# Expert weights dealt to partitions in runs of neighbouring rows, and the transposes that go with it

## The chip, the cores and the metric

One core of a Trainium2 chip runs the whole program. The metric is the device time of one execution in microseconds (us), the median of several; lower is better. Before the change it is 2893.73 us (three runs, 2891.6 to 2898.68).

## The reference

One layer of a decoder trunk for a prompt of 1024 tokens and 8 sample tokens (1032 tokens of 1024 features, all in float32): layer norm, adaptive modulation, an input projection, two mixing branches (a short gated convolution and a state-space scan), a merge, a second layer norm, and then a mixture of 32 experts, of which each token uses two. The change is in the experts alone. A token's features `xblk` meet two weight matrices of its expert:

```python
D_MODEL, D_EXPERT, N_EXPERTS, MOE_BLOCK = 1024, 512, 32, 128
# w_moe_13: (N_EXPERTS, D_MODEL, 2 * D_EXPERT)     w_moe_2: (N_EXPERTS, D_EXPERT, D_MODEL)
def expert_block(args):
    xblk, e = args
    gate, up = jnp.split(xblk @ w13[e], 2, axis=-1)
    return (jax.nn.silu(gate) * up) @ w2[e]
```

The tokens are sorted by expert into blocks of up to 128, and the two results of a token are added with their router weights. What is summed over is the feature axis (1024 in the first product, 512 in the second); the order of that sum is free.

## The kernel before

The program is written by hand for the five engines, each with its own list of instructions and semaphores between them; no scheduler moves anything. Up to about 2087 us it does the norms, projections, convolution, scan and merge. Then the router picks the experts (to about 2150 us), and the expert loop runs until about 2800 us: one turn for each block of 128 gathered token rows, 32 turns in the profiled run. After it the results are gathered back, scaled, normed and stored.

The weights of an expert are 6 MB: `w_moe_13[e]` is 1024 x 1024, loaded in four parts of 1 MB (`load_w13`, L635), and `w_moe_2[e]` is 512 x 1024, loaded in two (`load_w2`, L639). Part x of the first holds the 256 feature rows 256x to 256x + 255: row (2x + k) * 128 + p goes to partition p, column block k (k = 0, 1). So each partition gets two runs of 4 KB (one row of 1024 float32 each), and the part as a whole is one block of 1 MB in memory. SP issues all these loads; six buffers (`wraw`, called u_whole or arena in the rows) take them, and SP issues the next load into a buffer when DVE has last read it (`wlo_ready`).

Each raw part is split into two float32r halves: ACT copies it (`w_high`, L1062), DVE subtracts (`w_low`, L1559); a ring of three split buffers (we_parts) passes them to TensorE, which gives a buffer back with `wparts_used`. TensorE makes three matmuls for each product (high x high, high x low, low x high), in `gate_up` (L2092 to L2094) and `down` (L2110, L2113, L2114).

The token rows come by an indirect DMA from POOL into `xg` (tokens on partitions). TensorE wants the features on partitions, so it transposes them in blocks of 128 columns: `turn_rows` (L2079) makes four transposes into bank 6 for each half, and for each half ACT copies the result (`x_high`, L1067) and DVE takes the low part (`x_low`, L1661). The product h = silu(gate) * up (`silu` on ACT, L1071; DVE, L1666) is transposed in the same way by `turn_h` (L2120, four transposes into bank 7; `h_high` L1075, `h_low` L1670). Transpose k takes columns k * 128 to k * 128 + 127, the features of the rows that column block k of the weights holds. In a transpose the block that is turned is the loaded operand (LDWEIGHTS, shown as PEld), and the identity matrix is the one that is streamed (MATMUL, shown as PE).

TensorE's order in a turn n (`expert_turn`): the first half of gate/up part 0 of block n, `turn_h` of block n - 1, the second half of that part, `down` of block n - 1, gate/up part 1, the first half of the next token rows (`turn_rows`), part 2, the second half of them, part 3. ACT's order: `silu`, `w_high` 2, `h_high`, `w_high` 3 and 4, the two output copies (L1082, L1083) and their store, `w_high` 5, `x_high` of the first half, `w_high` 0 of the next block, `x_high` of the second half, `w_high` 1. DVE's: the product h, `h_low`, `w_low` 2 to 5, `x_low`, `w_low` 0, `x_low`, `w_low` 1.

Of the kernel before, what the change touches and what calls it, by code (L numbers as in the profile page):

```python
# [25 lines left out]
ds = bass.ds  # L26

P = 128
D = 1024
KD = D // P  # L30
# [69 lines left out]
def build(nc, t, o):  # L100
# [3 lines left out]
    with ctx:  # L104
        def sem(name):
            return ctx.enter_context(nc.semaphore(name))
# [24 lines left out]
        bank6, bank7 = pair[:, 0:512], pair[:, 512:1024]  # L131
# [7 lines left out]
        class Room:  # L139
# [5 lines left out]
            def take(self, n):  # L145
# [13 lines left out]
        ident = keep.take(P)  # L159
# [153 lines left out]
        hm = [r5.take(D_EXP) for _ in range(2)]  # L313
        xg = [r5.take(D), wflat[6]]
# [15 lines left out]
        wraw = [u_whole[:, 0:2 * D], w2_raw, r5.take(2 * D)] + [u_whole[:, 2 * D * x:2 * D * x + 2 * D]  # L330
                                                               for x in range(1, 4)]
# [52 lines left out]
        wraw_landed = [sem(f"wraw_landed{j}") for j in range(6)]  # L384
# [32 lines left out]
        def tile_rows(ap, i):  # L417
            return ap[i * P:(i + 1) * P, :] if i < TILES else ap[SEQ:TOK, :]

        w13_v = t["w_moe_13"][0].rearrange("e (k p) c -> p (e k) c", p=P)  # L420
        w2_v = t["w_moe_2"][0].rearrange("e (k p) c -> p (e k) c", p=P)

        def slots_before(n):

# [14 lines left out]
        def _(sp):  # L439
# [143 lines left out]
            with sp.Fori(0, 3) as i:  # L583
                c = sp.snap(i * 256)
# [47 lines left out]


            def load_w13(j, x, expert):
                sp.dma_start(wraw[j].rearrange("p (k c) -> p k c", k=2),  # L635
                             w13_v[:, ds(expert * KD + 2 * x, 2), :]).then_inc(wraw_landed[j], 16)

            def load_w2(x, expert):
                sp.dma_start(wraw[1 + x].rearrange("p (k c) -> p k c", k=2),  # L639
                             w2_v[:, ds(expert * 4 + 2 * x, 2), :]).then_inc(wraw_landed[1 + x], 16)  # L640


            sp.wait_ge(wo_done, TILES + 1)
            for x, j in enumerate((0, 3, 4, 5)):
                load_w13(j, x, 0)
            sp.wait_ge(x0_used, TILES + 1)
            load_w2(0, 0)
            sp.wait_ge(logits_done, 1)
            load_w2(1, 0)
            for x, j in enumerate((0, 3, 4, 5)):  # L650
                sp.wait_ge(wlo_ready, x + 1)
                load_w13(j, x, 1)
# [4 lines left out]
            def expert_of(n):  # L657
                return sp.value_load(plan[:, ds(n, 1)], min_val=0, max_val=EXPERTS - 1)

            with sp.Fori(0, extra + (PAIRS - 1)) as i:  # L660
                for b in range(2):
                    n = i * 2 + (b + 2)
                    before, expert = expert_of(i * 2 + (b + 1)), expert_of(i * 2 + (b + 2))
                    for j in range(6):
                        sp.wait_ge(wlo_ready, i * 12 + (6 * b + 5 + j))
                        if j in (1, 2):
                            load_w2(j - 1, before)
                        else:
                            load_w13(j, max(j - 2, 0), expert)
            expert = expert_of(extra * 2 + (2 * PAIRS - 1))  # L670
# [1066 lines left out]
        def _(pe):  # L1737
            pe.wait_ge(consts_ready, 1)
            pe.wait_ge(c_landed, 32)
            for k in range(KD):  # L1740
                last = pe.transpose(bank6[:, k * MROWS:(k + 1) * MROWS], crow[:, k * P:(k + 1) * P],
                                    ident[0:MROWS, 0:MROWS])
# [25 lines left out]
            for k in range(16):  # L1768
                last = pe.transpose(bank6[:, k * MROWS:(k + 1) * MROWS], mod[:, k * P:(k + 1) * P],
                                    ident[0:MROWS, 0:MROWS])  # L1770
# [3 lines left out]
            for k in range(KD):  # L1774
                last = pe.transpose(bank6[:, k * ROWS_C:(k + 1) * ROWS_C], rows_c[:, k * P:(k + 1) * P],
                                    ident[0:ROWS_C, 0:ROWS_C])
            last.then_inc(cols_turned, 1)
            for half in range(2):
                pe.wait_ge(cols_copied, 2 + half)
                for k in range(16):  # L1780
                    kk = 16 * half + k
                    last = pe.transpose(bank6[:, k * ROWS_S:(k + 1) * ROWS_S], rows_s[:, kk * P:(kk + 1) * P],
                                        ident[0:ROWS_S, 0:ROWS_S])
# [9 lines left out]
            for i in range(TILES + 1):  # L1793
                rows = P if i < TILES else NS
                for k in range(KD):
                    last = pe.matmul(bank7[0:rows, i * HEADS:(i + 1) * HEADS], uT[:, k, i * P:i * P + rows],
                                     w_dt[:, k, :], start=(k == 0), stop=(k == KD - 1))
# [242 lines left out]
            for i in range(TILES + 1):  # L2040
# [3 lines left out]
                for half in range(2):  # L2044
                    for k in range(KD):
                        last = pe.matmul(banks[2 * (i % 2) + half][0:rows, :], merged[:, k, i * P:i * P + rows],  # L2046
                                         w_o[:, k, 512 * half:512 * half + 512], start=(k == 0), stop=(k == KD - 1))
# [17 lines left out]
            for a in range(2 * NI):  # L2065
                last = pe.matmul(banks[4][:, 0:NBX], oh_lo[:, a, :], oh_hi[:, a, :], start=(a == 0),
                                 stop=(a == 2 * NI - 1))
# [3 lines left out]
            def turn_rows(b, n, half, landed):  # L2071

                if half == 0:
                    pe.wait_ge(xg_landed[b], landed)
                if not (isinstance(n, int) and n == 0 and half == 0):
                    pe.wait_ge(xt_ready, n * 2 + half)
                for k in range(4):
                    kk = 4 * half + k
                    last = pe.transpose(bank6[:, k * P:(k + 1) * P], xg[b][:, kk * P:(kk + 1) * P], ident)  # L2079
                last.then_inc(xg_turned, 1)  # L2080

            def gate_up(b, n, x, j, ks=(0, 1)):
# [34 lines left out]
            def turn_h(b, n):  # L2117
                pe.wait_ge(h_ready, n + 1)
                for k in range(4):
                    last = pe.transpose(bank7[:, k * P:(k + 1) * P], hm[b][:, k * P:(k + 1) * P], ident)  # L2120
                last.then_inc(ht_turned, 1)

            def expert_turn(b, n, landed):


                first = isinstance(n, int) and n == 0
                pe.wait_ge(xt_ready, n * 2 + 2)
                if first:
                    gate_up(b, n, 0, 0).then_inc(wparts_used, 1)
                else:  # L2130
                    if not (isinstance(n, int) and n == 1):
                        pe.wait_ge(h_ready, n - 1)
                    gate_up(b, n, 0, 0, (0,))
                    turn_h(1 - b, n - 1)
                    gate_up(b, n, 0, 0, (1,)).then_inc(wparts_used, 1)
                    if not (isinstance(n, int) and n == 1):
                        pe.wait_ge(o_free, n * 2 - 2)
                    down(1 - b, n - 1, 0, 2, n * 6).then_inc(wparts_used, 1)
                    down(1 - b, n - 1, 1, 0, n * 6 + 1).then_inc(wparts_used, 1)
                skip = 0 if first else 2  # L2140
                gate_up(b, n, 1, 1 + skip).then_inc(wparts_used, 1)
                turn_rows(1 - b, n + 1, 0, landed)
                gate_up(b, n, 2, 2 + skip).then_inc(wparts_used, 1)
                turn_rows(1 - b, n + 1, 1, landed)
                gate_up(b, n, 3, 3 + skip).then_inc(wparts_used, 1)
# [3 lines left out]
            for half in range(2):  # L2149
                turn_rows(0, 0, half, 16)  # L2150
            expert_turn(0, 0, 16)
            expert_turn(1, 1, 32)
            with pe.Fori(0, extra + (PAIRS - 1)) as i:
                expert_turn(0, i * 2 + 2, i * 16 + 32)
                expert_turn(1, i * 2 + 3, i * 16 + 48)
            turn_h(1, extra * 2 + (2 * PAIRS - 1))
            pe.wait_ge(o_free, extra * 4 + (4 * PAIRS - 2))
            down(1, extra * 2 + (2 * PAIRS - 1), 0, 2, extra * 12 + (12 * PAIRS)).then_inc(wparts_used, 1)
# [28 lines left out]
```

## Time and profile before

| | before |
|---|---|
| median of 3 runs | 2893.73 us (2891.6 to 2898.68) |
| the profiled execution | 2899.79 us, of it 2898.0 us from first to last instruction |
| mean granted TensorE clock | 0.952 |
| PE / PEld busy | 2587.1 us (89%) / 1892.4 us (65%) |
| DVE / ACT / POOL busy | 1506.0 us (52%) / 1051.9 us (36%) / 287.9 us (10%) |
| DMA | 405.11 MB, mean 140 GB/s |

The page describes this one execution. Its busy shares are means over stages that work differently, so the expert loop has to be looked at by itself: by the windows from 2184 to 2798 us. A "wait" in the tables is idle time of an engine and what ended it; the chain is followed back from an end to what released each step. PE's rows are matmuls, PEld's the loads of the operand that stays in the array.

### The profile page before, as it was taken

Reading aid. Unit: us, or ns where it says so; the run is one execution under the profiler, and the core shown is the slowest. Engines: PE = TensorE matmul, PEld = TensorE weight load, DVE = VectorE, ACT = ScalarE, POOL = GpSimd, SP = SyncE. Lnnn points to the kernel's source line nnn. Section 1 sums busy time; section 2 is a strip of 40 time slices with the busy share of each in tenths; the row PEclk is TensorE's granted clock in tenths of the full one; section 3 lists DMA queues with packets and bytes.
Section 4 is the critical chain, followed back from the end, with each engine's and each line's share of the span. In section 5 each row is a group of like instructions: output and inputs, shape, how many; then the busy total and the mean of one; then the engine's idle time right before and its main releaser. Section 6 shows DMA issues by size and latency. Waiting matters only on the chain.

```text
span 2898.0 us, 34179 instructions
## 1 busy us (share of the span) xinstructions
PE 2587.1 (89%) x11876; PEld 1892.4 (65%) x11876; DVE 1506.0 (52%) x2335; ACT 1051.9 (36%) x1338; POOL 287.9 (10%) x218
## 2 busy tenths in 40 slices
PE   6999999999999976899999999999949898988960
PEld 2376666666666644677789998875437777777750
DVE  3332576666765766100012331115557777777769
ACT  0212645535446445200000000000027777777751
POOL 0000000000000000111133441110000000000011
PEclk9889999999999988999999999999969999999985
DMA  8733222222222111111111112121239999999964
GB/s 272 260 117 102 74 62 60 69 71 64 62 68 71 55 39 33 46 44 43 43 31 51 43 50 103 44 54 66 102 119 352 368 358 361 364 356 368 362 242 142
DMA packets 253304, 405.11 MB, mean 140 GB/s; under 512 B 13273, under 2 KB 163425, under 8 KB 253161
## 3 DMA queue, kind: packets, MB, share of 16 engines
q1 hardware_dynamic: 227936, 327.72, 33.6%
q0 software_dynamic: 11744, 43.35, 4.1%
q10 hardware_dynamic: 13536, 33.04, 3.3%
q8 instruction: 35, 0.57, 0.1%
q14 instruction: 53, 0.43, 0.0%
HBM read 356.21 MB, written 48.15 MB: 140 GB/s over the span
## 4 chain that ended last, share of the span: by engine, by line
PE 41%; DVE 6%; issue 6%; ACT 5%; DMA 1%; ACTq 1%; DVEq 0%; POOL 0%; POOLq 0%; SPq 0%
PE bank L1974 11%; PE bank L1936 5%; PE bank L1938 5%; PE bank L1937 5%; PE bank L2046 4%; ACT we_parts L1062 4%; PE bank L2113 2%; PE bank L2110 2%; PE bank L2114 2%; DVE we_parts L1559 2%; PE bank L2079 1%; PE bank L2120 1%; DVE arena L1666 1%; DVE x_parts L1661 1%; ACT arena L1083 1%
## 5 line engine op out<-in xcount | busy, mean ns | idle before, releaser
L1810 PE MATMUL bank<-u_whole,arena 128*128 128x344 f32 x2304 | 693.0, 457 | 0.0
L1810 PEld LDWEIGHTS bank<-u_whole,arena 128*128 128x128 f32 x2304 | 436.2, 192 | 220.6 <-issue 15.0
L1559 DVE TENSOR_TENSOR we_parts<-u_whole,we_parts 128x2048 fp32r<-128x2048 f32 x129 | 295.1, 2287 | 79.2 <-ACT we_parts L1062 79.2
L1936 PE MATMUL bank<-u_parts,w_parts 128*128 128x344 f32 x960 | 313.0, 326 | 14.4 <-DVE u_parts L1418 7.3
L1937 PE MATMUL bank<-u_parts,w_parts 128*128 128x344 f32 x960 | 307.8, 321 | 0.0
L1974 PE MATMUL bank<-arena 128*128 128x344 f32 x1056 | 307.8, 452 | 0.0
L1938 PE MATMUL bank<-u_parts,w_parts 128*128 128x344 f32 x960 | 307.7, 321 | 0.0
L1062 ACT ACTIVATE we_parts<-u_whole 128x2048 fp32r<-128x2048 f32 x129 | 246.9, 1915 | 70.4 <-PE bank L2110 27.0
L1974 PEld LDWEIGHTS bank<-arena 128*128 128x128 f32 x1056 | 200.1, 190 | 101.8
L2092 PE MATMUL bank<-we_parts,x_parts 128*128 128x512 f32 x512 | 209.7, 410 | 3.3 <-DVE we_parts L1559 1.9
L2094 PE MATMUL bank<-we_parts,x_parts 128*128 128x512 f32 x512 | 201.1, 393 | 0.0
L2093 PE MATMUL bank<-we_parts,x_parts 128*128 128x512 f32 x512 | 200.4, 391 | 0.0
L1936 PEld LDWEIGHTS bank<-u_parts,w_parts 128*128 128x128 f32 x960 | 181.9, 189 | 17.9 <-DVE u_parts L1418 7.8
L943 ACT ACTIVATE arena<-bank 128x344 f32<-128x344 f32 x141 | 64.4, 456 | 336.1 <-PE bank L1810 326.8
L1937 PEld LDWEIGHTS bank<-u_parts,w_parts 128*128 128x128 f32 x960 | 181.5, 189 | 1.3
L1938 PEld LDWEIGHTS bank<-u_parts,w_parts 128*128 128x128 f32 x960 | 181.8, 189 | 0.0
L997 ACT ACTIVATE arena<-bank 128x344 f32<-128x344 f32 x48 | 22.0, 457 | 436.6 <-PE bank L1938 436.6
L1430 DVE TENSOR_TENSOR u_whole<-arena,bank 128x344 f32 (+1 forms) x24 | 12.3, 512 | 282.1 <-PE bank L1974 268.7
L1559 DVE TENSOR_TENSOR we_parts<-arena,we_parts 128x2048 fp32r<-128x2048 f32 x64 | 146.3, 2286 | 12.1 <-ACT we_parts L1062 12.1
L745 POOL TENSOR_TENSOR w_parts<-w_whole,one 128x1024 fp32r<-128x1024 f32 x40 | 76.7, 1918 | 641.9 <-PE bank L1938 618.4
L2046 PE MATMUL bank<-arena,u_whole 128*128 128x512 f32 (+1 forms) x288 | 125.0, 592 | 1.3 <-DVE u_whole L1483 1.3
L1297 DVE SCALAR_TENSOR_TENSOR arena<-arena 128x1023 f32<-128x1023 f32 (+2 forms) x96 | 122.5, 1276 | 0.0
(319 smaller groups left out, 3680.3 us busy)
## 6 DMA issues: line engine op xcount, KB each, us to landing
u_whole<-in_w_moe_dram SPq DMA_DIRECT2D x128, 1024.0 KB, 8.2
arena<-in_w_moe_dram SPq DMA_DIRECT2D x64, 1024.0 KB, 7.0
arena<-in_w_ada_dram SPq DMA_DIRECT2D x12, 2048.0 KB, 10.2
arena<-in_w_in_dram SPq DMA_DIRECT2D x48, 512.0 KB, 3.9
w_whole<-in_w_in_dram SPq DMA_DIRECT2D x40, 512.0 KB, 3.9
rows_dram<-arena ACTq DMA_DIRECT2D x32, 512.0 KB, 7.1
arena<-cum_dram ACTq DMA_DIRECT2D x62, 256.0 KB, 3.2
rows_dram<-u_whole POOLq DMA_DIRECT2D x2, 4096.0 KB, 21.1
```

Of the source, the lines that this page charges most:

```text
L1062: act.activation(w_his[parts_of(n, j)], wraw[slot], ACT.Copy).then_inc(whi_ready, 1)
L1297: last = dve.scalar_tensor_tensor(dst[:, back:SEQ], src[:, 0:SEQ - back], w(3 - back), dst[:, back:SEQ], ALU.mult, ALU.add)
L1559: dve.tensor_tensor(w_los[v], wraw[slot], w_his[v].bitcast(F32), ALU.subtract).then_inc(wlo_ready, 1)
L1810: last = pe.matmul(banks[part][:, 0:SUB], wslot[u][:, k, :], uT[:, k, part * SUB:(part + 1) * SUB], start=(k == 0), stop=(k == KD - 1))
L1936: pe.matmul(out, w_hi[v][:, k, :], u_hi[:, k, at], start=(k == 0), stop=False)
L1937: pe.matmul(out, w_hi[v][:, k, :], u_lo[:, k, at], start=False, stop=False)
L1938: last = pe.matmul(out, w_lo[v][:, k, :], u_hi[:, k, at], start=False, stop=(k == KD - 1))
L1974: last = pe.matmul(banks[3 + part][:, 0:SUB], wslot[out_slots[h][k // KD][0]][:, k % KD, :], src[:, k, part * SUB:(part + 1) * SUB], start ...
L2046: last = pe.matmul(banks[2 * (i % 2) + half][0:rows, :], merged[:, k, i * P:i * P + rows], w_o[:, k, 512 * half:512 * half + 512], start=( ...
L2092: pe.matmul(out, xt_hi[b][:, at], w_his[v][:, cols], start=(kk == 0), stop=False)
L2093: pe.matmul(out, xt_hi[b][:, at], w_los[v][:, cols], start=False, stop=False)
L2094: last = pe.matmul(out, xt_lo[b][:, at], w_his[v][:, cols], start=False, stop=(kk == KD - 1))
```

## The change

The rows of an expert's weights are dealt to the partitions differently. Of `w_moe_13[e]`, partition p now holds the eight neighbouring rows 8p to 8p + 7, and part x of a load brings rows 8p + 2x and 8p + 2x + 1, which are neighbours in memory: one run of 8 KB a partition instead of two of 4 KB. Of `w_moe_2[e]`, partition p holds the four rows 4p to 4p + 3, and each of the two parts brings two of them. A part is no longer one block of memory: its runs start 32 KB apart (16 KB for `w_moe_2`).

With that, column block k of a part stands for other features than before, and the transposed tokens have to match: transpose k of the token rows takes the columns k, k + 8, k + 16 and so on (128 of them, 8 words apart), and transpose k of h the columns k, k + 4, k + 8 and so on (4 words apart). Sizes, buffers, semaphores, and the order of instructions on every engine are the same.

```diff
-        w13_v = t["w_moe_13"][0].rearrange("e (k p) c -> p (e k) c", p=P)
-        w2_v = t["w_moe_2"][0].rearrange("e (k p) c -> p (e k) c", p=P)
+        w13_v = t["w_moe_13"][0].rearrange("e (p k) c -> p e (k c)", p=P)
+        w2_v = t["w_moe_2"][0].rearrange("e (p k) c -> p e (k c)", p=P)
...
             def load_w13(j, x, expert):
-                sp.dma_start(wraw[j].rearrange("p (k c) -> p k c", k=2),
-                             w13_v[:, ds(expert * KD + 2 * x, 2), :]).then_inc(wraw_landed[j], 16)
+                sp.dma_start(wraw[j].unsqueeze(1),
+                             w13_v[:, ds(expert, 1), 2 * D * x:2 * D * x + 2 * D]).then_inc(wraw_landed[j], 16)
 
             def load_w2(x, expert):
-                sp.dma_start(wraw[1 + x].rearrange("p (k c) -> p k c", k=2),
-                             w2_v[:, ds(expert * 4 + 2 * x, 2), :]).then_inc(wraw_landed[1 + x], 16)
+                sp.dma_start(wraw[1 + x].unsqueeze(1),
+                             w2_v[:, ds(expert, 1), 2 * D * x:2 * D * x + 2 * D]).then_inc(wraw_landed[1 + x], 16)
...
                 for k in range(4):
                     kk = 4 * half + k
-                    last = pe.transpose(bank6[:, k * P:(k + 1) * P], xg[b][:, kk * P:(kk + 1) * P], ident)
+                    last = pe.transpose(bank6[:, k * P:(k + 1) * P], xg[b].rearrange("p (t k) -> p k t", k=KD)[:, kk, :], ident)
                 last.then_inc(xg_turned, 1)
...
                 for k in range(4):
-                    last = pe.transpose(bank7[:, k * P:(k + 1) * P], hm[b][:, k * P:(k + 1) * P], ident)
+                    last = pe.transpose(bank7[:, k * P:(k + 1) * P], hm[b].rearrange("p (t k) -> p k t", k=4)[:, k, :], ident)
                 last.then_inc(ht_turned, 1)
```

## Rows read from the trace of the kernel before

**Rows 1.** The page: busy time by engine, then DMA share by 40 slices.
```profile
PE 2587.1 (89%) x11876; PEld 1892.4 (65%) x11876; DVE 1506.0 (52%) x2335; ACT 1051.9 (36%) x1338; POOL 287.9 (10%) x218
...
DMA  8733222222222111111111112121239999999964
```
**Rows 2.** Windows: us, busy us by engine (x instructions), granted clock, DMA share, GB/s.
```profile
2125.00:2150.00 25.00, 9.04 (x40) 8.47 (x40) 12.31 (x17) 0.60 (x1) 3.66 (x3) 0.50 0.36 126
...
2184.00:2798.00 614.00, 550.20 (x2541) 439.08 (x2539) 485.13 (x336) 439.22 (x363) 35.98 (x62) 1.00 0.97 359
```
**Rows 3.** Waits, 2250 to 2750 us: who waited for whom, us in total, times, longest.
```profile
ACT x_parts L1067 <- PE bank L2079: 34.7, 24, 1.4
...
PE bank L2120 <- DVE arena L1666: 32.4, 25, 1.3
...
ACT x_parts L1075 <- PE bank L2120: 22.8, 25, 0.9
```
**Rows 4.** The chain over one turn, 2401.9 to 2422.6: start us, us, what.
```profile
2401.79 0.47 PE bank L2110 x2
...
2404.07 1.92 ACT we_parts L1062
...
2408.37 0.61 DVE x_parts L1661
...
2409.03 0.67 PE bank L2079 x4
...
2412.16 2.29 DVE we_parts L1559
2414.45 0.61 DVE arena L1666
...
2415.11 0.66 PE bank L2120 x4
```
**Rows 5.** The chain over the whole loop: the same step of two turns.
```profile
2201.02 1.92 ACT we_parts L1062
...
2789.90 1.93 ACT we_parts L1062
```
**Rows 6.** A load and its reading: SP's and ACT's timelines, then lines L635 and L1062.
```profile
2401.38 10.35 SPq L635 DMA_DIRECT2D u_whole<-in_w_moe_dram  x4
...
2417.18 1.92 ACT L1062 ACTIVATE we_parts<-u_whole 128x2048 fp32r<-128x2048 f32 x1 [0.78 <-PE bank L2094]
...
DMA to landing us min/median/max: 4.8/8.2/10.7
...
L1062 ACT ACTIVATE we_parts<-u_whole x129: 1892/1917/1922, 2109.2 to 2792.2; 128x2048 fp32r<-128x2048 f32 x129
```
**Rows 7.** Window with six loads queued at once; columns as in rows 2.
```profile
2094.00:2104.00 10.00, 3.60 (x31) 3.18 (x31) 6.83 (x18) 1.80 (x4) 0.54 (x1) 0.50 1.02 410
```
**Rows 8.** Line L2079 in the loop: ns min/median/max, first and last start.
```profile
L2079 PEld LDWEIGHTS bank<-arena x193: 138/140/144, 2262.5 to 2749.9; 128*128 128x128 f32 x193
L2079 PE MATMUL bank<-arena x192: 270/272/334, 2262.7 to 2734.4; 128*128 128x128 f32 x192
```
**Rows 9.** PE's timeline: four transposes at 0.50 clock, unwaited, and after a wait.
```profile
2147.72 1.12 PE L2079 MATMUL bank<-arena 128*128 128x128 f32 x4 [9.83 <-DMA arena<-u_dram,arena]
...
2404.81 0.60 PE L2079 MATMUL bank<-arena 128*128 128x128 f32 x4
...
2409.03 0.66 PE L2079 MATMUL bank<-arena 128*128 128x128 f32 x4 [0.85 <-DVE x_parts L1661]
```
**Rows 10.** Two other lines' loads: of 9 columns, and the longest of 128.
```profile
L1751 PEld LDWEIGHTS bank<-arena x192: 87/91/141, 11.9 to 132.7; 128*9 128x9 f32 x192
...
L1796 PEld LDWEIGHTS bank<-arena,u_whole x144: 89/333/333, 135.8 to 164.0; 128*128 128x128 f32 x128, 128*8 128x8 f32 x16
```
**Rows 11.** DMA issues (gathers: 2250 to 2750 us): count, KB, median us to landing.
```profile
u_whole<-in_w_moe_dram SPq DMA_DIRECT2D x128, 1024.0 KB, 8.2
...
arena<-u_dram,arena POOLq DMA_INDIRECT x24, 7.9
```

## The prediction

> **What bounds the kernel now.** I began with the page. TensorE is busy for 89% of the span, and in the last fifth, the expert loop, the DMA line stands at 9 [rows 1]. That looks like a loop bound by its weight loads, which longer runs would help. The next views say otherwise. The windows give the loop's length (2184 to 2798 us, 614 us) and its load: DMA share 0.97, 359 GB/s, clock 1.00 [rows 2]. The waits of the loop, summed over 500 us, name only engines: ACT waits for PE, PE for DVE, DVE for ACT, and no DMA ends a wait of any of the three (those of the transposes are in [rows 3]). A loop fed too slowly would show ACT, which reads the raw weights, waiting for a landing.
>
> The chain over one turn of the loop says who does set the pace [rows 4]: the end of the down matmuls (PE L2110), ACT's two output copies, `w_high` on ACT, `x_low` on DVE, **four transposes of token rows (L2079)**, `x_high` and `w_high` on ACT, `w_low` and the gate product on DVE, **four transposes of h (L2120)**, then six gate/up and 24 down matmuls up to the next L2110. The turn repeats evenly: the same `w_high` starts at 2201.02 and, 29 turns later, at 2789.90 [rows 5], 20.31 us a turn.
>
> How far the loads stand from that chain shows in one slot. SP issues its load at 2401.38; L635's loads land at a median of 8.2 and at most 10.7 us after issue; ACT reads that slot at 2417.18 [rows 6]. So the data lies there 5 us or more before it is read. The transfers have a reserve of rate too: when six loads were queued at once the queue moved 410 GB/s [rows 7], against 359 in the loop, 14% more.
>
> **The change part by part.**
>
> *The loads.* All 192 loads keep their 1024 KB, place, order, queue and waits; only the runs grow from 4 to 8 KB, 128 instead of 256 a load. If a load gets quicker, it lands earlier in front of the 5 us reserve, and nothing waits for it: 0 us. At the loop's ends it is the same, since the first expert's six loads are moving at 2094 to 2104 us [rows 7] and the first is read at 2109.2 [rows 6]. If it gets slower, the reserve covers it until 1 MB costs 14% more of the queue's time than now. I put 0 for the loads; what would lie beyond the cover is a rival below.
>
> *The transposes.* Each turn has three groups of four: two for the next token rows (L2079, columns now 8 words apart), one for h (L2120, now 4 apart). Instructions and order on every engine stay; only the loaded operand's step changes. Now such a load takes 140 ns, its matmul 272, and the four matmuls follow each other every (0.60 - 0.27) / 3 = 0.11 us [rows 8, 9]. A load of 9 columns takes 91 ns [rows 10], so 119 words more cost 49 ns: 0.41 ns a word, the quickest read in the loop (ACT's `w_high` needs 1917 / 2048 = 0.94 ns a word, DVE's `w_low` 2.29 us / 2048 = 1.12) [rows 4, 6]. All these read neighbours; no row shows TensorE loading words that stand apart, so the price has to be bounded.
>
> From below: if the load keeps its pace, 0 us; a few ns slower it still hides under the 0.11 us of the matmul before it, and only the first load of a group shows. Nothing in the change gives a transpose less to do, which excludes a gain in this term. From above: the longest load of 128 columns that the trace has is 333 ns (L1796) [rows 10]. Less the 91 ns start that would be 242 ns of streaming, 0.13 us over the 0.11 us step for three of a group and 0.19 for the first: 0.58 us a group. Between them stands the one row in which these same four transposes run at half rate: before the loop, with the granted clock at 0.50 [rows 2], the group took 1.12 us against 0.66 with a full clock [rows 9], 0.45 more (a step of some 0.21 us, 1.7 ns a word). I take this one: 1.7 ns a word is four times 0.41, as if each word now cost what four neighbours cost, and the load then sets the step. It is a choice, and the largest doubt in the sum.
>
> At this place the Trainium skill speaks against the change: Advanced Engine Details and Errata, Memory Cachelines, says that SBUF is read in lines of 16 bytes and that a read wants at least two hits on a line to hide the access; words 32 and 16 bytes apart get one each. Vector Engine (DVE) Microarchitecture Reference, Measured stream behaviour on trn2, has 1.73 ns instead of 1.05 for a VectorE source that hops every element; as an estimate from that page, 128 x 1.73 = 0.22 us a load, 0.50 us a group, 32 us in all. No run here shows either yet, and neither page has a figure for TensorE.
>
> *What of it lies on the path.* The first half of the token rows (2404.81) does not: behind it PE has 0.85 us of waiting before the second half [rows 9], and ACT is in `w_high` from 2404.07 to 2405.99 before it can take the result [rows 4], so 0.45 us more is covered. Above 0.85 us a group it would no longer be. The second half does: ACT's `x_high` waits for it (34.7 us in 24 waits [rows 3]), and behind that are queued on ACT `w_high`, and on DVE `w_low` and the gate product that the h transposes need. The h group does: after it the six gate/up and 24 down matmuls follow without a gap, and ACT's `h_high` waits for it as well (22.8 us in 25 waits) [rows 3, 4]. A later down end pushes the next turn's output copies, so the delay is not given back. That is two groups a turn.
>
> *Sum.* 32 turns (L635 issues 128 loads, four a turn [rows 11]) x 2 groups x 0.45 us = 28.8 us. Ends: 0 and 32 x 2 x 0.58 = 37 us. Loads 0. The profiled execution took 2899.79 us (span 2898.0) and would go to 2929; the median of the runs shown is 2893.73, 6 us lower, and with the same term gives **2923 us**, 1.0% slower.
>
> **The rivals.**
>
> 1. *The separated words cost nothing that shows* (not slower). A load that doubles its streaming, 91 + 2 x 49 = 189 ns, still streams in 0.10 us and fits under the 0.11 us step; only the group's first pays 0.05 us: 64 x 0.05 = 3 us, so 2894 to 2897. For it: PE loads the next operand during the matmul before. Against it: the step is so short that nothing dearer fits. It decides as soon as the load streams in less than 0.11 us.
>
> 2. *The loads become the bound.* A load now takes 128 pieces 32 KB apart (w_moe_13; 16 KB in w_moe_2), where before it took one block of 1 MB. If memory served that worse by more than 14%, landings would take the place of PE in the turn. At 300 GB/s a turn's 20.31 x 359 = 7.3 MB take 24.3 us: +4.0 x 32 = 128 us, 3020 us. Against it: the gathers of token rows (4 KB each, scattered) already run in the mix, land in 7.9 us at the median and make nothing wait [rows 3, 11]. For it: only that no row has this pattern. The skill's DMA: Bandwidth & Descriptors, Latency and other measured facts, tells of lost rate at row pitches of 2 MiB and more and little or none at 512 KiB; by that 32 KB is harmless.
>
> 3. *Faster.* It would need a landing on the chain, and rows 3 and 4 have none; or engines that run quicker beside fewer, longer packets. `w_high` takes 1892 ns at its quickest and 1917 at the median [rows 6]: 0.025 us, twice a turn on the chain, 32 turns, at most 2 us. So 2892, within what can be measured.
>
> 4. *Words apart cost more than half rate*, beyond any row: at a 0.32 us step a group grows by some 0.9 us, the first half is covered no longer, and 32 x 2 x 0.9 = 58 us gives 2951.
>
> **How the numbers follow.** Forecast 0.52 (its own range 2912 to 2931, for 0.28 to 0.58 us a group); rival 1 0.30; rival 2 0.04; rival 3 0.06; rival 4 0.08. About 0.3% (9 us) is what a measurement of this kernel can tell from no change, so 2885 to 2902 is the same. Slower is the forecast with rivals 2 and 4, 0.64; the same is rival 1, 0.30; faster gets the 0.06 of rival 3, all of it for what rows 3 and 4 may not show, since the 2 us that I can price there would read as the same. The range for 8 in 10 starts just under the unchanged time (2889) and ends at 2945, past the upper end of the bound (2893.73 + 37 = 2931), short of rivals 2 and 4.
>
> **What would show it.** Right: loads of L2079 and L2120 of some 0.23 us or more instead of 140 ns, the unwaited group of four at about 1.05 us instead of 0.60, the turn at 21.2 us instead of 20.31, the loop's windows longer by 25 to 30 us with everything before 2087 us unchanged, DMA share and GB/s in the loop lower by the same 4%, and still no landing among the waits. If the loads stay at 140 to 190 ns and the turn at 20.3, rival 1 holds. If ACT L1062 waits for `u_whole<-in_w_moe_dram`, rival 2 does. The forecast is wrong altogether if the turn gets shorter than 20.3 us: then the loads were on the path in a way that the waits don't show.

## The result, and the profile after

The changed kernel takes 2902.49 us (median of 20 runs, 2897.5 to 2906.53) against 2896.18 us for the kernel before in as many runs beside it (2891.6 to 2899.2). The ratio is 1.0022, with a 95% interval of 1.0016 to 1.0028: 6.3 us longer (4.6 to 8.1). That is more than nothing and less than the 0.3% that the prediction named as the bound of a difference that can be told. The forecast was 29 us. The profiled execution of the kernel after took 2906.53 us, 6.7 us more than that of before.

First the page and the windows of the kernel after, with the columns of [rows 1, 2]:

```profile
PE 2592.1 (89%) x11876; PEld 1899.1 (65%) x11876; DVE 1505.9 (52%) x2335; ACT 1051.9 (36%) x1338; POOL 290.6 (10%) x218
...
DMA  7733222222222111111111113111239999999964
```

```profile
2094.00:2104.00 10.00, 5.77 (x40) 5.35 (x40) 7.03 (x13) 2.52 (x6) 0.54 (x1) 0.51 1.01 424
...
2184.00:2798.00 614.00, 550.19 (x2526) 442.72 (x2525) 480.72 (x330) 436.41 (x361) 34.82 (x60) 1.00 0.95 357
```

The loop looks as before: clock 1.00, TensorE as busy, DMA share 0.95 for 0.97. With six loads queued the queue moved 424 GB/s for 410 (one window of 10 us each). What changed is in the loads of the two transpose lines (ns min/median/max, 2250 to 2750 us), 138/140/144 before [rows 8]:

```profile
L2079 PEld LDWEIGHTS bank<-arena x194: 185/191/208, 2249.9 to 2740.8; 128*128 128x128 f32 x194
...
L2120 PEld LDWEIGHTS bank<-arena x100: 195/209/222, 2255.8 to 2747.0; 128*128 128x128 f32 x100
```

What a dearer load costs is read from PE's timeline: from the first of a group of four to the matmul that stands behind it. The kernel before has these followers (the groups start at 2404.81, 2409.03 and 2415.11 in [rows 4, 9]):

```profile
2405.16 0.48 PE L2092 MATMUL bank<-we_parts,x_parts 128*128 128x512 f32 x1
...
2409.44 0.48 PE L2092 MATMUL bank<-we_parts,x_parts 128*128 128x512 f32 x1
...
2415.52 0.48 PE L2092 MATMUL bank<-we_parts,x_parts 128*128 128x512 f32 x1
```

And the kernel after, in a turn of the same place:

```profile
2409.05 0.60 PE L2079 MATMUL bank<-arena 128*128 128x128 f32 x4
2409.41 0.48 PE L2092 MATMUL bank<-we_parts,x_parts 128*128 128x512 f32 x1
...
2413.27 0.71 PE L2079 MATMUL bank<-arena 128*128 128x128 f32 x4 [0.87 <-DVE x_parts L1661]
2413.74 0.47 PE L2092 MATMUL bank<-we_parts,x_parts 128*128 128x512 f32 x1
...
2419.40 0.74 PE L2120 MATMUL bank<-arena 128*128 128x128 f32 x4 [1.31 <-DVE arena L1666]
2419.90 0.48 PE L2092 MATMUL bank<-we_parts,x_parts 128*128 128x512 f32 x1
```

The group that follows other matmuls without a wait costs 0.36 us for 0.35. The second half of the token rows, which starts after a wait, costs 0.47 for 0.41, and the h group 0.50 for 0.41. The two that stand on the chain, and wait, thus pay 0.06 and 0.09 us: 0.15 us a turn.

Where in the group it falls is read from the start of the second transpose, that is of the last three. Before:

```profile
2409.20 0.49 PE L2079 MATMUL bank<-arena 128*128 128x128 f32 x3
...
2415.27 0.49 PE L2120 MATMUL bank<-arena 128*128 128x128 f32 x3
```

And after:

```profile
2413.48 0.50 PE L2079 MATMUL bank<-arena 128*128 128x128 f32 x3
...
2419.62 0.52 PE L2120 MATMUL bank<-arena 128*128 128x128 f32 x3
```

From the first transpose of a waiting group to its second it was 0.17 us and is 0.21 (token rows) and 0.22 (h). The steps behind it hardly change: by the single records of 24 or 25 such groups, the median step between the other transposes goes from 0.109 us to 0.113 (token rows) and 0.120 (h).

The chain over the loop gives the turn. Its first and last `w_high` (start us, us, what), kernel before:

```profile
2164.45 1.91 ACT we_parts L1062
...
2796.04 1.92 ACT we_parts L1062
```

The same two steps after:

```profile
2166.99 1.91 ACT we_parts L1062
...
2803.03 1.92 ACT we_parts L1062
```

From 631.59 to 636.04 us: 4.45 us more over some 31 turns (631.59 / 20.31), 0.14 us a turn, close to the 0.15 of the two groups. The other 2.5 us of the two profiles lie ahead of 2164.45, where both kernels run the same instructions; below, two kernels reach that step at 2158.5 and 2159.45, so the start scatters by more than this. The waits of the kernel after (2250 to 2750 us) are those of [rows 3], ACT's two longer by just this:

```profile
ACT x_parts L1067 <- PE bank L2079: 37.6, 25, 1.5
...
ACT x_parts L1075 <- PE bank L2120: 25.1, 25, 1.0
```

1.45 us a wait became 1.50 for the token rows, 0.91 became 1.00 for h. No DMA ends a wait of PE, DVE or ACT in the loop, before or after.

### The profile page after: what moved, and what is told of

Same layout as the page of the kernel before. It is cut to its first block, busy times and chain, and to the rows that moved or that the text cites. A ratio compares the mean times of both kernels' runs of the same rounds, so it can differ in the third digit from the quotient of the medians.

```text
span 2904.8 us, 34179 instructions
## 1 busy us (share of the span) xinstructions
PE 2592.1 (89%) x11876; PEld 1899.1 (65%) x11876; DVE 1505.9 (52%) x2335; ACT 1051.9 (36%) x1338; POOL 290.6 (10%) x218
## 4 chain that ended last, share of the span: by engine, by line
PE 41%; DVE 7%; issue 6%; ACT 5%; DMA 1%; ACTq 1%; POOL 0%; DVEq 0%; POOLq 0%; SPq 0%
PE bank L1974 11%; PE bank L1936 5%; PE bank L1938 5%; PE bank L1937 5%; PE bank L2046 4%; ACT we_parts L1062 4%; PE bank L2113 2%; PE bank L2110 2%; PE bank L2114 2%; DVE we_parts L1559 2%; PE bank L2079 1%; PE bank L2120 1%; DVE arena L1666 1%; DVE x_parts L1661 1%; ACT arena L1083 1%
## 5 line engine op out<-in xcount | busy, mean ns | idle before, releaser
L1062 ACT ACTIVATE we_parts<-u_whole 128x2048 fp32r<-128x2048 f32 x129 | 246.9, 1915 | 70.3 <-PE bank L2110 26.6
L2092 PE MATMUL bank<-we_parts,x_parts 128*128 128x512 f32 x512 | 209.2, 409 | 3.3 <-DVE we_parts L1559 1.9
```

What stands on the lines that cost most here:

```text
L1062: act.activation(w_his[parts_of(n, j)], wraw[slot], ACT.Copy).then_inc(whi_ready, 1)
L2092: pe.matmul(out, xt_hi[b][:, at], w_his[v][:, cols], start=(kk == 0), stop=False)
```

## The experiments

Two questions were open: is all of the 4.45 us the transposes', with the loads worth nothing; and why do loads that are a third to a half longer show so little? The theory is rival 1's mechanism: the matmul ahead of a transpose (0.11 us a step) hides the longer load, so only the first load of a group that waits pays, and the h loads stick out a little. Its rivals: the 8 KB runs bring something that the transposes take away again; or the price depends on what was read (h or token rows), and not on the step.

| kernel | first to last `w_high` of the chain | against before | load L2079 / L2120, ns | ratio of times (95%) |
|---|---|---|---|---|
| before | 631.59 us | | 140 / 140 | |
| after | 636.04 | +4.45 | 191 / 209 | 1.0022 (1.0016 to 1.0028) |
| loads_only | 631.55 | -0.04 | 140 / 141 | 0.9999 (0.999 to 1.0008) |
| turns_only | 636.04 | +4.45 | 191 / 210 | 1.0016 (1.0007 to 1.0025) |
| x_only | 633.10 | +1.51 | 191 / 141 | 1.0005 (0.9996 to 1.0014) |
| h_only | 634.32 | +2.73 | 140 / 209 | one run, 2894.95 us |
| x_four | 634.06 | +2.47 | 208 / 140 | one run, 2894.29 us |
| pairs | 637.06 | +5.47 | 208 / 210 | 1.0012 (1.0003 to 1.0021) |

**loads_only** has the new loads with the old transposes.

```diff
-        w13_v = t["w_moe_13"][0].rearrange("e (k p) c -> p (e k) c", p=P)
-        w2_v = t["w_moe_2"][0].rearrange("e (k p) c -> p (e k) c", p=P)
+        w13_v = t["w_moe_13"][0].rearrange("e (p k) c -> p e (k c)", p=P)
+        w2_v = t["w_moe_2"][0].rearrange("e (p k) c -> p e (k c)", p=P)
...
+                sp.dma_start(wraw[j].unsqueeze(1),
+                             w13_v[:, ds(expert, 1), 2 * D * x:2 * D * x + 2 * D]).then_inc(wraw_landed[j], 16)
...
```

> The 8 KB loads alone, with the transposes of before (features then meet other features' weights, so the output is not the reference's). Theory E (only the transposes cost, by the part of their loads that no matmul hides: 0.145 us a turn, 4.5 us in all; the loads cost nothing): the time of before, turn 20.31 us, loads of L2079 and L2120 at 140 ns. Rival L (the 8 KB pieces 32 KB apart carry a share of the 6.3 us, the 1.8 us that the turns of the loop don't explain): +1.8 us or more, turn 20.36 us or longer, or w_high and w_low slower.

2896.41 us, 0.9999 of the kernel before. The chain's loop is as long as before:

```profile
2158.50 1.91 ACT we_parts L1062
...
2790.05 1.92 ACT we_parts L1062
```

The queue's work did get a little less. In 500 us of the loop (queue, packets, MB, share of 16 engines) the weight queue of loads_only shows

```profile
q1 hardware_dynamic: 21256, 154.82, 82.6%
...
u_whole<-in_w_moe_dram SPq DMA_DIRECT2D x99, 1024.0 KB, 8.0
```

Half the packets and 82.6% of the engines' time, for as many MB as turns_only, below, has in 83.8%. The time goes nowhere: a load that lands at 8.0 us instead of 8.2 [rows 11] lands in front of a reserve of 5 us.

**turns_only** has the old loads with the new transposes.

```diff
-                    last = pe.transpose(bank6[:, k * P:(k + 1) * P], xg[b][:, kk * P:(kk + 1) * P], ident)
+                    last = pe.transpose(bank6[:, k * P:(k + 1) * P], xg[b].rearrange("p (t k) -> p k t", k=KD)[:, kk, :], ident)
...
-                    last = pe.transpose(bank7[:, k * P:(k + 1) * P], hm[b][:, k * P:(k + 1) * P], ident)
+                    last = pe.transpose(bank7[:, k * P:(k + 1) * P], hm[b].rearrange("p (t k) -> p k t", k=4)[:, k, :], ident)
```

> The strided transposes alone, with the loads of before (output not the reference's, for the same reason). Theory E: +4.5 us, turn 20.45 us, loads of L2079 at 191 and of L2120 at 209 ns, the granted clock of the loop 1.00. Rival L: less than +3 us here, the rest with the loads. A second rival (longer loads cost more without the quicker landings of the 8 KB runs): more than +6.3 us.

2900.63 us, 1.0016 (+4.6 us, between 2.0 and 7.2). Its queue and its chain:

```profile
q1 hardware_dynamic: 40103, 154.63, 83.8%
```

```profile
2159.45 1.91 ACT we_parts L1062
...
2795.49 1.92 ACT we_parts L1062
```

636.04 us, to the hundredth what the whole change has. So the transposes are all of the cost in the loop, and the loads give none of it back.

**x_only** and **h_only** each make one of the two pairs of load and transpose: `w_moe_13` with the token rows, `w_moe_2` with h.

x_only:

```diff
-        w13_v = t["w_moe_13"][0].rearrange("e (k p) c -> p (e k) c", p=P)
+        w13_v = t["w_moe_13"][0].rearrange("e (p k) c -> p e (k c)", p=P)
...
+                    last = pe.transpose(bank6[:, k * P:(k + 1) * P], xg[b].rearrange("p (t k) -> p k t", k=KD)[:, kk, :], ident)
```

h_only:

```diff
-        w2_v = t["w_moe_2"][0].rearrange("e (k p) c -> p (e k) c", p=P)
+        w2_v = t["w_moe_2"][0].rearrange("e (p k) c -> p e (k c)", p=P)
...
+                    last = pe.transpose(bank7[:, k * P:(k + 1) * P], hm[b].rearrange("p (t k) -> p k t", k=4)[:, k, :], ident)
```

> The change for w_moe_13 and the token rows alone; w_moe_2 and h as before (same output as the reference). Theory E: only the second half of the token rows lies on the chain, 0.054 us a turn: turn 20.36 us, +1.7 us; the first half's loads are as dear (191 ns) and cost nothing. Rival (both halves on the chain, since PE runs behind by as much): 0.11 us a turn, +3.4 us.

> The change for w_moe_2 and h alone (same output as the reference). Theory E: the h group grows by 0.088 us and all of it is on the chain: turn 20.40 us (x_only had 20.354 against 20.308, and the two must add up to the 20.451 of the whole change, which asks for 20.405). Rival (the two delays overlap, since both feed the same chain): a turn of 20.43 us or more.

x_only took 2897.39 us, 1.0005; h_only 2894.95 us in its one run, beside seven of the kernel before at 2893.19 to 2900.02, so its total tells nothing and only its trace is used. The chains, x_only:

```profile
2161.58 1.92 ACT we_parts L1062
...
2794.68 1.92 ACT we_parts L1062
```

and h_only:

```profile
2158.45 1.91 ACT we_parts L1062
...
2792.77 1.92 ACT we_parts L1062
```

+1.51 and +2.73 us, together 4.24 of the 4.45. Of 12 loads in a turn that grew, the eight of the token rows cost 0.05 us (1.51 / 31) and the four of h 0.09. So the cost doesn't follow the number of loads, as a load that sets the step would have it.

**x_four** asks whether the step or the buffer makes h dearer: the token rows at 4 words apart, as h has it, and h as before.

```diff
-        w13_v = t["w_moe_13"][0].rearrange("e (k p) c -> p (e k) c", p=P)
+        w13_v = t["w_moe_13"][0].rearrange("e (h p k) c -> p (e h) (k c)", p=P, k=4)
...
+                    last = pe.transpose(bank6[:, k * P:(k + 1) * P], xg[b].rearrange("p (h t k) -> p h k t", h=2, k=4)[:, kk // 4, kk % 4, :], ident)
```

> w_moe_13 dealt in two halves of 512 rows, four neighbouring rows a partition: 8 KB runs 16 KB apart, token rows transposed with columns 4 words apart; w_moe_2 and h as before (same output as the reference). If the step sets the price of a load: L2079 at 209 ns, as h has at 4 words (8 words: 191), its second half 0.09 us longer, turn 20.40 us. If it is the tile or its place (hm against xg) and not the step: 191 ns, turn 20.354 as in x_only.

One run, 2894.29 us (before beside it 2892.6 to 2900.03): again only the trace speaks. Its loads at L2079 and its chain:

```profile
L2079 PEld LDWEIGHTS bank<-arena x197: 195/208/222, 2256.2 to 2749.9; 128*128 128x128 f32 x197
```

```profile
2157.91 1.91 ACT we_parts L1062
...
2791.97 1.92 ACT we_parts L1062
```

The same line and buffer go from 191 to 208 ns when the words stand 4 apart instead of 8, and the loop from +1.51 to +2.47 us. The step decides, not what is read, and of these two the wider step is the cheaper one.

**pairs** keeps the 8 KB runs and deals rows so that the columns are only 2 words apart, in both transposes. (It has two lines fewer, so its lines are 2 lower.)

```diff
+        w13_v = t["w_moe_13"][0].rearrange("e (x p k) c -> p (e x) (k c)", p=P, k=2)
+        w2_v = t["w_moe_2"][0].rearrange("e (x p k) c -> p (e x) (k c)", p=P, k=2)
...
+                    last = pe.transpose(bank6[:, k * P:(k + 1) * P], xg[b].rearrange("p (x t k) -> p x k t", x=4, k=2)[:, kk // 2, kk % 2, :], ident)
```

> Another deal with 8 KB runs: partition p of part x holds rows 256x + 2p and 256x + 2p + 1, so a part is again one block of 1 MB, and the transposes take every second column, 2 words apart (same output as the reference). If a load is slowed by getting one word of each 16 bytes, two words a 16-byte line are enough: loads at 140 ns, turn 20.31 us, the time of before. If any step above one word slows it: loads of 185 ns or more, turn 20.45 us, +4.5 us. Either way no gain from the 8 KB runs, as nothing waits for a landing.

2899.9 us, 1.0012 (1.0003 to 1.0021). Its loads of the token rows and its chain:

```profile
L2077 PEld LDWEIGHTS bank<-arena x192: 194/208/224, 2258.5 to 2734.4; 128*128 128x128 f32 x192
```

```profile
2159.71 1.91 ACT we_parts L1060
...
2796.77 1.92 ACT we_parts L1060
```

Two words apart cost what four cost, and the loop is the longest of all (+5.47). The median of its time lies under that of the kernel after while its loop is 1 us longer; that is the size of what the medians can't tell, and why the loop's length is read from the chain. The Trainium skill (Advanced Engine Details and Errata, Memory Cachelines) would have the pairs cheaper, since two words 8 bytes apart share a line of 16 bytes; the loads of TensorE don't bear that out here: 208 ns with two on a line, 208 to 209 with one, 191 with one on every other line.

**short_4k, short_8k, short_pairs** were to make the loads bind: of three matmuls for each product only high x high stays, so the low parts are left out of both expert products. short_4k has the old loads and transposes, short_8k those of the change, short_pairs those of pairs.

```diff
-                        pe.matmul(out, xt_hi[b][:, at], w_his[v][:, cols], start=(kk == 0), stop=False)
-                        pe.matmul(out, xt_hi[b][:, at], w_los[v][:, cols], start=False, stop=False)
-                        last = pe.matmul(out, xt_lo[b][:, at], w_his[v][:, cols], start=False, stop=(kk == KD - 1))
+                        last = pe.matmul(out, xt_hi[b][:, at], w_his[v][:, cols], start=(kk == 0), stop=(kk == KD - 1))
```

> The kernel before with only the high x high matmuls in the experts (24 a turn instead of 72; the low parts are still made but not used, so the output is coarser). This takes 20 matmuls of 0.227 us, 4.5 us, off the chain of a turn: 15.8 us would be left, DVE's busy time is 16.0 us a turn, and the queue needs 7.3 MB / 410 GB/s = 17.8 us. Theory Q (the reserve of the loads is 14%, then the queue binds): turn 17.8 us, ACT now waiting for landings of w_moe, time some 2.5 x 31 = 78 us under before, about 2819 us. Rival (the queue has more to give, engines bind): turn 16 to 16.5 us, no waits for landings.

> The same cut on the changed kernel. Theory Q, with the 424 GB/s that six queued loads moved after the change: turn 17.2 us, so 0.6 us a turn and some 18 us under short_4k: what the longer runs are worth where the loads bind. Rival (longer runs win nothing in a steady mix with gathers and stores): turn as in short_4k within 0.1 us, or longer by the transposes' 0.14 us.

> The same cut on the kernel with 8 KB runs in one block of 1 MB (rows 256x + 2p and 256x + 2p + 1 on partition p, transposes with columns 2 words apart). If run length sets the rate: turn as in short_8k. If pieces 32 KB apart cost rate that an unbroken block does not: shorter than short_8k by more than 0.1 us a turn.

2863.88, 2864.64 and 2867.02 us: 1.0 to 1.1% under the kernel before, and alike among themselves. Both expectations for the turn missed, 17.8 us and 16 to 16.5 us: that of short_4k came down only to 19.6 us (by the starts of its `w_high`), and still no landing ended a wait. Its loop (columns of [rows 2]) and two of its groups (L2114 is its `turn_h`) show where part of the cut time went:

```profile
2250.00:2700.00 450.00, 291.74 (x828) 184.23 (x828) 365.73 (x252) 330.75 (x276) 26.56 (x45) 0.67 0.99 374
```

```profile
2407.09 1.12 PE L2079 MATMUL bank<-arena 128*128 128x128 f32 x4 [2.87 <-DVE x_parts L1661]
...
2413.63 1.12 PE L2114 MATMUL bank<-arena 128*128 128x128 f32 x4 [2.83 <-DVE arena L1666]
```

With its matmuls gone TensorE waits 2.8 us ahead of each such group, the granted clock falls from 1.00 to a mean of 0.67, and the transposes take 1.12 us, as before the loop at a clock of 0.50, the lower of the two levels (1.2 of 2.4 GHz) [rows 2, 9]. Part of the work taken off one engine came back as a slower clock on the same engine; how much of the 3.8 us a turn that the cut didn't give (4.5 less 0.7) is the clock's was not measured. The three runs say nothing of what loads that bind are worth; a bound has to be made by adding bytes.

**more_4k and more_8k** do that: SP issues two more transfers of 1 MB a turn, from `w_moe_2` to a memory of their own, with the old (4k) and the new (8k) loads and transposes. Nothing of the computation changes.

```diff
+        more_dram = nc.dram_tensor("more_dram", (2 * (PAIRS + OVER // 2) * 512, D), F32, kind="Internal").ap()
...
+                        if j in (2, 5):
+                            sp.dma_start(more_dram[ds(i * 1024 + (512 * b + 256 * (j // 3)), 256), :],
+                                         t["w_moe_2"][0, 0, 0:256, :]).then_inc(more_done, 16)
```

> The kernel before plus two copies of 1 MB a turn inside the chip's memory, on SP's queue behind the loads (same output): a load on the queue, none on the engines. Theory Q (at some 410 GB/s the queue binds): a turn moves 7.3 + 2.1 = 9.4 MB, 22.9 us, +2.6 us x 30 = 78 us, and ACT's w_high now waits for landings of w_moe. Rival (the copies are dearer or cheaper than loads by the byte): another turn, but still set by landings.

> The same two copies a turn added to the changed kernel. Theory Q with the packets' durations (309 ns for 8 KB against 2 x 159 for 4 KB): six loads of 1 MB take 2.485 instead of 2.55 us each, so a turn 0.39 us shorter than in more_4k, 12 us in all: what the longer runs are worth once the queue binds, and the transposes' 0.14 us is hidden then. Rival (8 KB runs gain nothing in the mix): the same turn within 0.1 us.

2963.16 us (1.0235, 1.0218 to 1.0252) and 2956.17 us (1.0209, 1.0192 to 1.0226), of four runs each: the intervals overlap, but every run of more_8k is under every run of more_4k. Window, waits and chain of more_4k (lines behind the added ones are 7 higher, so L1069 is `w_high`):

```profile
2250.00:2750.00 500.00, 413.31 (x1849) 316.13 (x1848) 356.35 (x243) 320.50 (x264) 25.55 (x44) 1.00 1.02 420
```

```profile
ACT we_parts L1069 <- DMA u_whole<-in_w_moe_dram: 112.6, 62, 2.8
...
ACT we_parts L1069 <- DMA arena<-in_w_moe_dram: 43.6, 44, 1.3
```

```profile
2157.82 1.91 ACT we_parts L1069
...
2856.75 1.92 ACT we_parts L1069
```

and of more_8k, whose strided loads at the transposes are as long as those of the change (185/191/208 ns):

```profile
2250.00:2750.00 500.00, 421.89 (x1875) 325.70 (x1876) 360.03 (x245) 324.65 (x267) 25.65 (x44) 1.00 1.01 425
```

```profile
ACT we_parts L1069 <- DMA u_whole<-in_w_moe_dram: 108.1, 67, 2.9
...
ACT we_parts L1069 <- DMA arena<-in_w_moe_dram: 35.3, 44, 1.0
```

```profile
2161.76 1.91 ACT we_parts L1069
...
2851.77 1.92 ACT we_parts L1069
```

This is how a loop that its loads bind looks: ACT, the first reader, waits for landings in 106 places of 500 us, 156 us in all, and the clock stays at 1.00. Here the 8 KB runs do help: 425 GB/s for 420, and the same stretch of the chain takes 690.01 us for 698.93, 8.9 us less (7.0 by the medians; 12 were expected). A turn in the steady part takes 22.74 us in more_4k, where 22.9 was expected, and 22.43 in more_8k, 0.31 less where 0.39 was expected. The sign of the change depends on which of the two is on the chain.

## Why the prediction was wrong, point by point

**What bounds the loop: right.** No landing is on the chain, and the loads were put at 0: loads_only has 631.55 us for 631.59. The DMA share of 0.97, which looks like a bound, wasn't one; it took two more transfers a turn to make it one.

**The loads: right.** The runs 32 KB apart are served no worse: landings at 8.0 us for 8.2, 424 GB/s for 410 with six queued. With that rival 2 is out. The sentence of the Trainium skill that was weighed against it (DMA: Bandwidth & Descriptors, Latency and other measured facts) has pitches from 512 KiB up; that 16 and 32 KB do no harm is shown by these runs alone, and they are in line with it.

**Which groups pay: right.** The first half of the token rows is covered (0.36 us for 0.35), the second half and h are not, and the delay isn't given back: 0.06 + 0.09 us a turn at the groups, 0.14 at the turn.

**The price of a load: the step that failed.** The term was 32 turns x 2 groups x 0.45 us = 28.8 us. The 0.45 came from a streaming of 1.7 ns a word, four times the old 0.41, taken from the row in which the same transposes run at half the clock; the load was then to set the step. Measured, 119 words more than the 9-column load take (191 - 91) / 119 = 0.84 ns a word 8 apart and (209 - 91) / 119 = 0.99 ns 4 apart: 2.0 and 2.4 times the old price, not four. And this price falls just where it is hidden: 191 - 91 = 100 ns of streaming lies under the step of 0.11 us, 118 ns sticks out by some 0.01 us. So a waiting group pays the growth of its first load, some 0.05 us, and h pays 0.01 us more for each of its other three; the term is 31 turns x (0.06 + 0.09) = 4.7 us, and the chain has 4.45.

The half-clock row was the wrong neighbour: there all of TensorE ran at half rate, matmuls too, so it says nothing of a load that slows beneath a matmul at full speed. The upper bound has the same fault, which the prediction doesn't say: the 333 ns of L1796 stand at a granted clock of 0.50. The trace of before had a nearer row, at a clock of 1.00, that was not read: the router's matmuls of 36 columns (L2035), each with a load of 128 columns of its own. The windows of the two lines and L2035's loads:

```profile
140.00:160.00 20.00, 20.00 (x96) 20.00 (x95) 0.00 (x0) 0.00 (x0) 0.00 (x0) 0.50 0.41 115
...
1980.00:2090.00 110.00, 110.00 (x379) 55.21 (x378) 61.04 (x74) 8.28 (x18) 3.72 (x7) 1.00 0.16 56
```

```profile
L2035 PEld LDWEIGHTS bank<-arena x112: 186/192/192, 1989.1 to 2089.4; 128*128 128x128 f32 x112
...
1989.51 1.75 PEld L2035 LDWEIGHTS bank<-arena 128*128 128x128 f32 x15 [0.24 <-issue]
```

Loads of 192 ns follow each other there every (1.75 - 0.19) / 14 = 0.11 us. They read neighbouring words, so the row doesn't price words apart; but it shows that a load longer by 50 ns than a transpose's needs no longer step. The prediction had this working in rival 1, doubled streaming and 189 ns a load, and gave it 0.30, with "the step is so short that nothing dearer fits" against it.

By the estimate from the Trainium skill (Vector Engine (DVE) Microarchitecture Reference, Measured stream behaviour on trn2) a load would take 0.22 us. The trace has 0.19 and 0.21, so the load was near. The 0.50 us a group that was made of it was not: it takes the whole 0.22 us as streaming, with the 91 ns start on top, which would be a load of 0.31 us; measured, 0.10 and 0.12 us are streaming.

**The forecast's signs.** A load of 0.23 us or more (by the forecast's own step of 0.21 us it would be 0.3), an unwaited group of 1.05 us and a turn of 21.2 us: none came (0.19 to 0.21, 0.60, 20.45). Those of rival 1 nearly did: 191 and 209 ns against 140 to 190, a turn of 20.45 us against 20.3, 0.09 us instead of 0.05 for the h group. Its 3 us were 4.45 in the loop. The time itself, 2902.49 us, lies in the range of 2889 to 2945, but that range began under the unchanged time; 2902 is rival 1's part of it and not that of the forecast's 29 us.

**What stays open.** The medians differ by 6.3 us (4.6 to 8.1) and the loop explains 4.45. The 2 us between are not in the profiled loops: the stretch before it, where the kernels run the same instructions, ends anywhere from 2158 to 2167 us in these profiles. Times differ with TensorE's mean granted clock, which is not the same in every execution of one kernel (0.950 to 0.954). At the same clock the 20 runs of the kernel after are 3.7 to 5.2 us longer than the 47 of the kernel before that were run beside the experiments: medians of 2905.57 against 2901.45 us at 0.950, 2901.86 against 2897.85 at 0.952, 2899.88 against 2895.24 at 0.954. That fits the 4.45 of the loop and leaves little else. Whether the 20 runs had a slightly lower clock (0.9521 in the mean, against 0.9525) by chance or by the change is not shown.

None of the versions that keep all three matmuls of a product is shown to beat the kernel before; the short ones do, by 1.0 to 1.1%, with a coarser output.

## What to carry to other kernels

A dearer operand load costs only what the matmul ahead of it doesn't hide, and the first of each group that starts after a wait: count the groups on the chain that wait, not the loads. A busy queue is not a bound: look for a landing among the waits, and for the reserve between landing and reading, before bytes or runs are made cheaper. To see what loads are worth when they do bind, add bytes; taking matmuls away lowered TensorE's clock here, from 1.00 to 0.67, and answered another question.

## What the runs showed of the hardware that was not expected

- In these transposes TensorE's load of 128 columns of 128 float32 takes 140 ns from neighbouring words, 208 to 210 ns from words 2 or 4 apart and 191 ns from words 8 apart. Each of the three steps costs, and the widest costs least. The 140 ns are not the price of every load of neighbours: before other matmuls a load of this size takes 188 ns (L2092 in the loop) and 192 (L2035), at a clock of 1.00.
- Loads in 8 KB runs take the queue 1.5% less of its engines' time than in 4 KB runs (82.6% for 154.82 MB, 83.8% for 154.63), and it moves 425 GB/s for 420 where it binds. SP's own issue of one got shorter too, 333 for 373 ns (L635, medians in the loop).
- Without two thirds of its matmuls TensorE was granted 0.67 of its clock (mean of 450 us) instead of 1.00, and of the work removed 0.7 us a turn was left as gain (20.3 to 19.6).
